# Hybrid diffusion layer on one core: two buffers for the masked blocks of the scan's doubling steps

## The reference

```
def step(S, inp):
    r_t, w_t, k_t, v_t, kk_t, a_t = inp
    sa = jnp.einsum('bhij,bhj->bhi', S, -kk_t)
    S = (S * w_t[:, :, None, :] + sa[..., None] * (kk_t * a_t)[:, :, None, :]
         + v_t[..., None] * k_t[:, :, None, :])
    y = jnp.einsum('bhij,bhj->bhi', S, r_t)
    return S, y
```

## Time and profile before

| | |
|---|---|
| three runs | 2633.46 us median (2632.03 to 2636.31) |
| the profiled execution, its own time | 2636.95 us |
| its span in the profile | 2635.1 us |
| busy over the span | PE 2426.6 us (92%), DVE 1012.2 us (38%), ACT 636.7 us (24%), POOL 359.1 us (14%) |
| mean granted TensorE clock | 0.966 |
| POOL on L672 | 200 instructions, 162.2 us busy |

### The profile page before, as it was taken

The page is one execution under the profiler, slowest core; times in us unless marked ns, Lnnn a source line. Parts: engine busy times, 40 slices in busy tenths (PEclk is TensorE's granted clock), DMA queues, the critical chain, the costliest instruction groups (busy, mean ns, idle before and its releaser), DMA issues. The chain is left out here.

```text
span 2635.1 us, 58505 instructions
## 1 busy us (share of the span) xinstructions
PE 2426.6 (92%) x26407; PEld 1546.8 (59%) x26407; DVE 1012.2 (38%) x1770; ACT 636.7 (24%) x1207; POOL 359.1 (14%) x402
## 2 busy tenths in 40 slices
PE   6999997698999989989799769999999999999997
PEld 4999995587787777778696423333333333333333
DVE  3344311658477576574345611212121212121214
ACT  2121222435445345343320101111111111111111
POOL 0000000315325134144002400000000000000000
PEclk8999998799999999999999879999999999999998
DMA  9363331010000000000092199999999999999984
GB/s 347 131 221 102 114 114 61 20 44 5 27 25 5 27 26 5 27 8 4 19 332 66 56 369 392 404 385 404 384 405 387 401 385 405 383 405 384 404 328 160
DMA packets 181023, 538.29 MB, mean 204 GB/s; under 512 B 13382, under 2 KB 54054, under 8 KB 180648
## 3 DMA queue, kind: packets, MB, share of 16 engines
q1 hardware_dynamic: 177704, 524.34, 52.2%
q0 software_dynamic: 2976, 10.16, 1.8%
q10 hardware_dynamic: 96, 0.05, 0.0%
HBM read 504.15 MB, written 30.38 MB: 203 GB/s over the span
## 5 line engine op out<-in xcount | busy, mean ns | idle before, releaser
L1818 PE MATMUL ps_h_lat<-w_piece,xT 128*64 128x512 f32 x2048 | 456.8, 599 | 10.7 <-DVE hidden L1944 7.5
L1818 PEld LDWEIGHTS ps_h_lat<-w_piece,xT 128*64 128x64 f32 x2048 | 146.0, 138 | 314.9 <-issue 314.9
L1938 DVE TENSOR_TENSOR hidden<-sigmoid_lat,ps_h_lat 64x1024 f32<-64x1024 f32 x32 | 39.1, 1223 | 506.5 <-ACT sigmoid_ctx L1711 506.5
L1843 PE MATMUL ps_y_lat<-w_piece,hiddenT 128*64 128x512 f32 x1024 | 232.6, 596 | 0.0
L1827 PE MATMUL ps_h_ctx<-w_piece,xT 128*16 128x512 f32 x2048 | 226.1, 593 | 0.0
L325 PE MATMUL ps_in<-hT_hi,w_in_hi 128*128 128x320 f32 x752 | 174.3, 313 | 2.6 <-issue 2.6
L672 POOL TENSOR_TENSOR Mo<-x,levels_sb 128x256 f32<-128x256 f32 x200 | 162.2, 834 | 99.2 <-PE ps_scan L914 99.1
L325 PE MATMUL ps_in<-hT_lo,w_in_hi 128*128 128x320 f32 x752 | 172.3, 310 | 0.0
L325 PE MATMUL ps_in<-hT_hi,w_in_lo 128*128 128x320 f32 x752 | 172.1, 310 | 0.0
L914 PE MATMUL ps_scan<-TT_diag,Mo 64*64 64x64 f32 x3200 | 117.3, 223 | 43.5 <-issue 27.2
L1843 PEld LDWEIGHTS ps_y_lat<-w_piece,hiddenT 128*64 128x64 f32 x1024 | 70.0, 137 | 137.7 <-issue 137.1
(11 more groups left out here) (310 smaller groups left out, 3580.2 us busy)
## 6 DMA issues: line engine op xcount, KB each, us to landing
w_piece<-in_w_e SPq DMA_DIRECT2D x192, 2048.0 KB, 15.8
w_ada<-in_w_ada SPq DMA_DIRECT2D x12, 2048.0 KB, 15.3
w_in_raw<-in_w_in SPq DMA_DIRECT2D x23, 1024.0 KB, 6.4
rkv_scratch<-projected SPq DMA_DIRECT2D x24, 320.0 KB, 6.4
rkv_T<-rkv_scratch SPq DMA_DIRECT2D x8, 960.0 KB, 5.4
gates_scratch<-projected SPq DMA_DIRECT2D x16, 320.0 KB, 6.8
gate_sb<-gates_scratch SPq DMA_DIRECT2D x8, 640.0 KB, 6.5
x<-in_x_sample SPq DMA_DIRECT2D x8, 512.0 KB, 12.3
```

Source lines behind the costliest of these rows:

```text
L1818: last = pe.matmul(psA[rows, cs], x[:, k, A], w[:, q, cs], start=(k == 0), stop=(k == KD - 1))
L1843: last = pe.matmul(psY[rows, :], hT[:, f, A], w[:, q, c * 512:(c + 1) * 512], start=(hf == 0 and f == 0), stop=(hf == 1 and f == FK - 1))
L1938: v.tensor_tensor(hid[A, :], sg[UP, :], psA[UP, :], ALU.mult)
```

## The change

`Mo` becomes two buffers, taken in turn by the level's parity. POOL's wait moves back by one level: blocks of level 3 wait until the products of level 1 are done, those of level 2 wait for nothing. The products and the masks are the same.

```
-        T, Z, Mo, TD = [sb(n, [P, NG, NPROB, HD]) for n in ("T", "Z", "Mo", "TT_diag")]
+        T, Z, TD = [sb(n, [P, NG, NPROB, HD]) for n in ("T", "Z", "TT_diag")]
+        Mo = [sb(f"Mo{n}", [P, NG, NPROB, HD]) for n in range(2)]
...
                     b, l = steps[n]
-                    if l > 1:
-                        g_.wait_ge(s_z, i * NS + n - NGR + 1)
+                    if l > 2:
+                        g_.wait_ge(s_z, i * NS + n - 2 * NGR + 1)
                     for p in range(*GROUPS[b]):
-                        ins = g_.tensor_tensor(Mo[:, p, :, :].rearrange("p (e h) n -> p e h n", e=2), Mq[:, ORDER[p], 0:2, :, :],
+                        ins = g_.tensor_tensor(Mo[l % 2][:, p, :, :].rearrange("p (e h) n -> p e h n", e=2), Mq[:, ORDER[p], 0:2, :, :],
                                                levels[:, l, :, :].unsqueeze(2).broadcast_to([P, 2, 2, HD]), ALU.mult)
                     ins.then_inc(s_mo, 1)
...
-                                last = pe.matmul(ps_of(b_z(b), b)[hs, c, q, :], Mo[hs, p, q, :], TD[hs, p, q, :], start=True, stop=True)
+                                last = pe.matmul(ps_of(b_z(b), b)[hs, c, q, :], Mo[l % 2][hs, p, q, :], TD[hs, p, q, :], start=True, stop=True)
```

## The result

| | before | changed |
|---|---|---|
| median, 20 runs each | 2632.59 us | 2636.66 us |
| lowest to highest | 2630.65 to 2636.31 | 2633.61 to 2641.34 |
| ratio, 95% interval | | 1.0015 (1.0009 to 1.0021) |
| profiled execution, its span | 2636.95, 2635.1 us | 2637.52, 2635.7 us |

A second comparison of the same pair (11 runs against 33) gave 1.0014 (1.0005 to 1.0023). So the change costs some 3 to 4 us: it lies within the 0.2% that was set as "same", but its interval leaves out zero. The changed time is 3.1 us above the forecast of 2633.6. The forecast stood on a time before of 2633.46 and the time before is now 2632.59, so the change itself cost 4.1 us where 0.15 was forecast.

The account below looks back on a forecast made before the run. PE bounds the scan; POOL's masks act only by slowing DVE. Six tiles of 0.84 loss less 0.76 gain, first tile -0.3, last 0, add 0.15 to 2633.46: 2633.6 us, range 2629.0 to 2640.0.

Parts of the forecast that it names:

- What bounds the kernel: In the scan's tiles PE is the bound; no product at levels 2 to 5 waits for its mask.
- The gain, 0.76 a tile: Before level 5, L1099 and L1107 run free of POOL, so PE's products start 0.76 us earlier.
- Rival (b): The wait before level 5 isn't DVE's: no gain, only loss, 2639.0 to 2642.3 us; chance 0.06.
- The loss, 0.84 a tile: At level 2 the last two first-direction scans meet POOL, 0.42 us more each, and the delay passes to PE.
- upper bound of 1.31: Most the level 2 loss could be: 0.84 us plus 0.47 for one more two-operand DVE operation meeting masks.
- The sum: Six tiles at +0.5 us in all, first tile -0.3, last 0: together +0.1 or +0.2 us.
- the accident: Fourth tile's addition L1235 starts after 0.43 us idle; taken as showing that level 2 delay, 0.6 us, stays to tile's end.
- (a): At level 2 POOL is late instead of the scans, leaving only the gain of 5.3 us: 2628.1; chance 0.08.
- (c): PE's new waits at level 2 bring its clock down, at most 1.5 us a stretch: 2639.6; chance 0.06.
- (d): At level 2 each of two scans waits a whole mask, loss 1.34 us a tile: 2637.1; chance 0.1.
- (e): Masks are ahead of PE anyway and contention only changes place, without effect on PE: 2633.5 us; chance 0.1.
- near draw: The forecast itself for the whole kernel: loss and gain nearly cancel, +0.1 or +0.2 us, 2633.6; chance 0.6.

Follow-up runs that it names:

- spilled masks: Kernel before, one buffer and old waits, plus five masks behind those of level 2 into a buffer nobody reads: 2642.96 against 2634.24 us, 1.0036.
- the old wait: Changed kernel's two buffers, but every level waits for the products of the level before it, as before: 2634.80 against 2634.24 us, 1.0002.
- the one with levels 4 and 5 early: Changed kernel's two buffers, but level 3 waits as before and only levels 4 and 5 run ahead: 2632.36 against 2634.24 us, 0.9994.
- the three kernels with the hold at the right mask: Third group's level 2 mask waits for DVE's second-group level 1 addition; on before 2632.89, changed 2631.89, levels 4 and 5 early 2631.99 us.

## Why the prediction was right or wrong

**What bounds the kernel: right.** No product waits for a mask of levels 2 to 5, before or after; POOL acts on PE only through DVE. The spilled masks show this by themselves.

**The gain, 0.76 a tile: right to the hundredth.** L1100 and L1108 are at 0.82 and 0.83, the products of level 5 follow on 0.14 after the engine's last one (751.89 + 0.63 to 752.66), and the distance from level 2 to level 5 has shrunk by 22.61 - 21.85 = 0.76. The second wait stays at 1.51. Rival (b) falls: the wait labelled "issue" was DVE's.

**The loss, 0.84 a tile: right in kind, too small.** The step that was too small is "2 x 0.42 = 0.84 us". It holds for the scans (0.85), but the term was taken as the scans alone. It measured 1.20, since the longer run of masks also met the operation behind the scans (0.24) and, by 0.11, the addition to `y_T`. The working let room for it in its upper bound of 1.31, but filled it with one more operation of two operands from SBUF. It was one with a single operand, which I had counted as safe. The rule of the Trainium skill (page "SBUF — State Buffer", section "Who interferes with whom") leaves the operations with one SBUF input out only where they don't run in a two-port mode, and names `tensor_scalar` and `copy` among those that can; the prediction gives the rule without this condition, and so more widely than the page states it. The trace agrees that such an operation pays: L1095 takes 0.17 us alone and 0.41 beside POOL. That it ran in such a mode, no run here shows. With 0.35 more on six tiles the forecast would have been 2633.6 + 2.1 = 2635.7.

**The sum.** Six tiles at 0.44 give +2.6. For the first, the loss is 102.97 - 102.73 = 0.24 (spilled masks against the old wait, both at full clock) and the gain 0.76: -0.5. The prediction had 0.42 for the loss of this tile. Together +2.1 of the +4.1 by the medians, or of the +3.1 of the second comparison. In the profiled execution the seven tiles sum to 722.58 against 719.28 us, +3.3: the four clean ones give +1.7, the first +0.5 at the same clock of 0.97, the fourth +1.34, the second -0.22. So the first tile did not win its 0.5 there; in the second trace of the changed kernel it is 104.16 us, 0.06 under before. The idle 0.43 of DVE in the fourth tile is not the accident that the prediction took it for: it is there again, at 0.42, in the fourth tile with the old wait, and the changed kernel taken again has a fourth tile of 103.35 at full clock, 0.47 more than before. The 0.87 above that in the first trace is a stretch of low clock; in the second tile it was before that had one. A steady cost outside the tiles is not seen: span less the seven tiles is 1913.1 and 1912.7 us in the two traces of the changed kernel, 1915.8 before and 1909.9 with the old wait. So one to two microseconds of the difference are not settled: they lie in stretches of low clock, or are the luck of the runs.

**The rivals.** (a), POOL gives way: no, all five scans are slow. (c), the clock: PE's new waits of 0.97 and 0.31 did not bring the clock down. Four of the five tiles shown are at 1.00. In the one at 0.98, the fourth tile of the scan, the granted clock is 1.00 from 828 to 832 us, behind these waits, and 0.61 from 858 to 862, behind the wait of 1.52 at level 5 that was there before. A part of the unsettled rest may be such stretches. (d), the exclusive port, gave 2637.1, nearest to the measured time, and for a wrong reason: a scan pays 0.42 and not the 0.67 of a whole mask. Of the lock for the whole length that the Trainium skill states (same page and section), the trace agrees that DVE's operations pay, not on how much. (e), nothing: no.

**The bounds and the chances.** 2636.7 lies in the range of 2629.0 to 2640.0, and the change is within 0.2%; but the "near draw" was a loss that can be measured. The range was wide enough to hold rival (d) as well as the forecast, and of the 3.9 us by which the change cost more than was forecast, the larger loss at level 2 explains some 2.

## What to carry to other kernels

An engine that is ahead of its reader costs nothing by waiting, and its waits can be worth something: here POOL's pause was what let DVE's scans run free. Before a producer is given a second buffer, ask not only who waits for it but beside what it will run, and list every operation of DVE in that stretch, the small ones and those of one operand too. Where it must be moved, move single pieces: the mask that is read last could be held back at no cost, and this one wait gave most of the shorter tile without the second buffer, while holding its neighbours as well made PE wait 0.83 us for them.

## What the hardware showed that was not expected

A VectorE operation with one operand in SBUF is slowed by GpSimd as well: TENSOR_SCALAR on 128x5 values from 0.17 to 0.41 us in the changed kernel, and in the one with levels 4 and 5 early TENSOR_SCALAR on 128x640 from 0.55 to 0.81 and a COPY of it from 0.49 to 0.80. The additions of 128x512 with an operand in PSUM stay at 0.68 or 0.69 in every tile shown, beside POOL or not. For the small one the wait is longer than the work, so the price is not a share of the length.

The scans pay far less than a mask's length each: five of 128x128 take 1.68 us free and 3.66 beside masks of 0.67 us, 0.40 more for each. The masks pay less still here: in the kernel with the spilled ones, the ten masks of this stretch take 0.67 to 0.79 us each, and 0.67 alone.

The same program at the same place in a tile can fall to the lower level of the clock for a stretch, or not: 0.65 of full speed on average over four microseconds in one tile and 1.00 in the other, behind the same waits of 0.20 and 1.52 us. In these single profiles a tile with such a stretch is 0.5 to 0.9 us longer, as much as most of what the experiments moved, and in the three kernels with the hold at the right mask it came in one to four of six tiles. In sixteen of the eighteen such tiles of all the traces, the first tiles left out, the stretch lies at level 5, where PE waits 1.52; in one it lies at level 4 and in one at level 3, where PE has waits of 1.83 and 1.72. What decides it was not tested.
